# Mixer slices loaded channels-first from a second copy of the input, with the pooled product moved behind the fourth up tile

## Chip, cores and metric

The kernel runs on one core of a Trainium2 chip. The metric is the device time of one execution in microseconds (us), over several runs. The version before the change takes 1790.71 us (median of 3 runs, 1789.93 to 1791.59).

## What is computed

One layer (DEPTH is 1) of an encoder on two sequences of 2048 and 512 tokens, 1024 channels, in float32, with the same weights:

```
h = rms_norm(x, g_mix)
y = pool_mixer(h, pool_w, pool_scale)
x = x + y
x = x + relu(rms_norm(x, g_mlp) @ w_up)**2 @ w_down      # 1024 -> 4096 -> 1024
out = rms_norm(x, g_fin)

def pool_mixer(h, w, scale):          # four groups of 256 channels, windows 2, 4, 8, 16 tokens
    mean = (sum of h over the window centred on t) / (tokens in the window)
    d = mean - h                      # per channel group
    return einsum('bsgc,gce->bsge', d, w) * scale
```

## The kernel before

**Groups and steps.** The 2560 tokens are handled in five groups of 512 (`GT`). The hidden layer of a group is walked in eight steps (`PAIRS`) of 512 of its 4096 columns, so there are 40 steps. TensorE (PE) does in step n four *up tiles* 4n to 4n+3 (24 matmuls of 512 columns each: every f32 product is made of three, hi*hi, lo*hi and hi*lo, from operands split into a rounded high part and a rest) and, for the step before, the seven *products* of a Strassen scheme with w_down, in the order P1, P5, P6, P3, P4, P7, P2 (12 matmuls each, `product`, L1188 to L1190). ScalarE (ACT) takes the relu and the square of an up tile (L533, L535) and writes the high parts; VectorE (DVE) writes the low parts (L756, L765, L773), forms the Strassen sums (L785 to L817), and adds every finished product to its sum in SBUF (`evict`, L832). In the first group the split of w_down is made by DVE and ACT too (`split_w`, `sum_w`) and stored to DRAM; later groups load it back.

**The ring.** Products leave PE through a ring of two pairs of PSUM banks (`ring_pair`). `ring_turns` gives each product its turn; turns alternate between the pairs. A matmul group with turn r waits until turn r-2 has been read (`ring_read`), which only DVE does, in its own order.

**The mixer of the next group** is made during the steps of the present one. At step 2 of a group (`STATS_STEP`) SP loads the next group's rows `xr` and halo rows `xh`, ACT takes their mean squares (`row_stats`) and GpSimd (POOL) the factors `rs_x`. In steps 3 to 6 (`WINDOW_STEP` + w, w = 0 to 3) one channel group of 256 each is mixed:

- ACT multiplies the slice by the row factors into `xw` (`norm_rows`, L553, one step ahead), PE transposes it to channels by tokens with eight transposes ahead of the step's first up tile and two for the halo ahead of the second (`turn_window` L1198, `turn_halos` L1205), ACT copies the result from PSUM to `ht` (L562, L569);
- POOL adds shifted copies, w+1 adds of about 128x1024 for window w and a small multiplication at the sequence ends (`window_sums`, L347, L354);
- DVE subtracts the slice itself (`subtract_own`, L887), ACT writes the high part `dt_hi` (L573), DVE the low part `dt_lo` (L892);
- PE multiplies by the mixer weights: 24 matmuls of 256 columns into two turns of the ring, two halves of 256 tokens each (`pool_out`, L1213 to L1215);
- DVE adds both halves to `xr` (`add_pooled`, L875).

In step 7 the mixed rows are normalised, and at the boundary PE transposes them for the next group's up tiles. The first group has a path of its own, which the change leaves alone; so four groups by four windows, 16 *window steps*, are concerned.

**What sets the order.** The instructions of every engine are written out by hand in the `step` functions, one per engine, and each engine runs its own in that order. In a window step PE's `step` is

```
turn_window; up_tile(4n); P1; P5; turn_halos; up_tile(4n+1); P6; P3; up_tile(4n+2); P4; P7
pool_out
up_tile(4n+3); P2
```

Of PE's turns, the two halves of the pooled product lie between P7 and P2: P7's pair is the one of the second half, and P2 goes to the pair of the first half. SP issues the loads of rows, weights and mixer weights (`pw_slot`), ACT those of w_up (`load_wu`, behind each `split_wu`).

## Time and profile before

| | |
|---|---|
| median of 3 runs | 1790.71 us |
| profiled execution | 1790.22 us |
| its span in the trace | 1788.4 us |
| PE busy | 1756.3 us, 98% of the span |
| DVE busy | 1122.7 us, 63% |
| ACT busy | 761.4 us, 43% |
| POOL busy | 158.7 us, 9% |
| mean granted TensorE clock | 0.996 |
| DMA | 432.67 MB, mean 242 GB/s |

The busy times are those of one execution. Each engine's time is the union of its instructions, so 98% of PE says that hardly a moment passes without a matmul in flight; it does not say where an added wait would sit. The 1.8 us between the span and the time of that execution lie around the traced span. Consecutive matmuls overlap: a row's duration is longer than the distance to the next start, and it is the distance that costs time. The same holds for DVE and ACT, where the next start comes some 0.08 us ahead of an end.

### The profile page before, as it was taken

The page shows a single profiled execution, that of the slowest core. Times are in us where ns is not written, and L with a number is a line of the kernel's source. Part 1 is how long each engine was busy: PE and PEld are TensorE (multiplying, and loading weights), DVE is VectorE, ACT ScalarE, POOL GpSimd, SP SyncE. Part 2 cuts the span into 40 slices and gives each one's busy share as a digit, 9 for nine tenths or more (in the row PEclk, how much of TensorE's full clock was granted, in tenths as well). Part 3 has the DMA queues.
Part 4 walks back from the last instruction along what each step waited for, and adds up shares of the span by engine and source line. Part 5 has one row for each costly group of instructions (what it writes and reads, how often), then busy time and mean ns, then how long its engine had stood idle before and what let it go on. Part 6 is the DMA issues. An engine that isn't in the chain of part 4 may idle for free.

```text
span 1788.4 us, 20968 instructions
## 1 busy us (share of the span) xinstructions
PE 1756.3 (98%) x8156; PEld 1461.8 (82%) x8156; DVE 1122.7 (63%) x1178; ACT 761.4 (43%) x1186; POOL 158.7 (9%) x139
## 2 busy tenths in 40 slices
PE   8999999999999999999999999999999999999996
PEld 8888887778888888888888888888888888888885
DVE  6678888786555564765555647645556575445447
ACT  6556554554343335344333344343333543233232
POOL 4000112001001120010011200000112010000001
PEclk9999999999999999999999999999999999999998
DMA  7597766668856665668666555776665657666654
GB/s 266 218 348 281 265 252 242 245 263 326 307 212 224 223 224 212 247 242 295 243 223 223 213 212 204 280 295 223 224 224 212 235 205 273 240 223 239 233 202 163
DMA packets 80902, 432.67 MB, mean 242 GB/s; under 512 B 8860, under 2 KB 10780, under 8 KB 42916
## 3 DMA queue, kind: packets, MB, share of 16 engines
q1 hardware_dynamic: 57764, 347.44, 52.6%
q10 hardware_dynamic: 23040, 83.90, 13.8%
q8 instruction: 65, 1.06, 0.2%
q14 instruction: 33, 0.27, 0.0%
HBM read 360.00 MB, written 71.30 MB: 241 GB/s over the span
## 4 chain that ended last, share of the span: by engine, by line
PE 89%; DVE 6%; ACT 1%; DMA 1%; issue 1%; POOL 1%; ACTq 0%; SPq 0%; POOLq 0%; DVEq 0%
PE up_ps L1169 16%; PE up_ps L1171 16%; PE up_ps L1170 16%; PE ring_ps L1188 13%; PE ring_ps L1190 13%; PE ring_ps L1189 13%; DVE m_acc L832 1%; PE ring_ps L1213 1%; DVE w_slot L765 1%; PE ring_ps L1215 1%; PE ring_ps L1214 1%; DVE a_slot L773 1%; PE mix_ps L1198 1%; DVE wu_lo L756 1%; DMA wd_raw<-w_down 1%
## 5 line engine op out<-in xcount | busy, mean ns | idle before, releaser
L756 DVE TENSOR_TENSOR wu_lo<-wu_raw,wu_hi 128x1024 fp32r<-128x1024 f32 x158 | 195.8, 1239 | 579.7 <-ACT wu_hi L496 579.7
L1169 PE MATMUL up_ps<-h_hi,wu_hi 128*128 128x512 f32 x1280 | 501.4, 392 | 0.6 <-DVE h_lo L897 0.6
L1171 PE MATMUL up_ps<-h_hi,wu_lo 128*128 128x512 f32 x1280 | 498.5, 389 | 0.0
L1170 PE MATMUL up_ps<-h_lo,wu_hi 128*128 128x512 f32 x1280 | 498.5, 389 | 0.0
L533 ACT ACTIVATE a_raw<-up_ps 128x512 f32<-128x512 f32 x160 | 95.3, 596 | 509.0 <-PE up_ps L1171 509.0
L832 DVE TENSOR_TENSOR m_acc<-ring_ps,m_acc 128x1024 f32<-128x1024 f32 x245 | 298.6, 1219 | 18.8 <-PE ring_ps L1190 18.4
L1188 PE MATMUL ring_ps<-w_slot,a_slot 128*128 128x512 f32 x760 | 296.8, 391 | 1.1 <-DVE m_acc L832 1.1
L1190 PE MATMUL ring_ps<-w_slot,a_slot 128*128 128x512 f32 x760 | 295.9, 389 | 0.0
L1189 PE MATMUL ring_ps<-w_slot,a_slot 128*128 128x512 f32 x760 | 295.7, 389 | 0.0
L1171 PEld LDWEIGHTS up_ps<-h_hi,wu_lo 128*128 128x128 f32 x1280 | 240.2, 188 | 50.5
L1169 PEld LDWEIGHTS up_ps<-h_hi,wu_hi 128*128 128x128 f32 x1280 | 240.3, 188 | 49.4 <-DVE h_lo L897 1.2
L1170 PEld LDWEIGHTS up_ps<-h_lo,wu_hi 128*128 128x128 f32 x1280 | 240.4, 188 | 48.3
L525 ACT CAST a_slot<-s_sum 128x512 fp32r<-128x512 f32 x160 | 99.4, 621 | 278.4 <-PE ring_ps L1190 98.5
L1188 PEld LDWEIGHTS ring_ps<-w_slot,a_slot 128*128 128x128 f32 x760 | 142.6, 188 | 31.1 <-issue 1.5
L1190 PEld LDWEIGHTS ring_ps<-w_slot,a_slot 128*128 128x128 f32 x760 | 142.6, 188 | 29.9
L1189 PEld LDWEIGHTS ring_ps<-w_slot,a_slot 128*128 128x128 f32 x760 | 142.7, 188 | 29.2
L496 ACT CAST wu_hi<-wu_raw 128x1024 fp32r<-128x1024 f32 x160 | 165.4, 1034 | 0.0
L1188 PE MATMUL ring_ps<-w_more,a_slot 128*128 128x512 f32 x360 | 140.6, 391 | 0.1
L1190 PE MATMUL ring_ps<-w_more,a_slot 128*128 128x512 f32 x360 | 140.2, 389 | 0.0
L1189 PE MATMUL ring_ps<-w_more,a_slot 128*128 128x512 f32 x360 | 140.1, 389 | 0.0
L773 DVE TENSOR_TENSOR a_slot<-s_sum,a_slot 128x512 fp32r<-128x512 f32 x160 | 134.1, 838 | 3.4 <-ACT a_slot L525 3.4
L525 ACT CAST a_slot<-a_raw 128x512 fp32r<-128x512 f32 x120 | 74.5, 621 | 104.6 <-PE ring_ps L1190 104.5
(136 smaller groups left out, 1642.2 us busy)
## 6 DMA issues: line engine op xcount, KB each, us to landing
w_slot<-w_cache SPq DMA_DIRECT2D x134, 1024.0 KB, 5.1
w_more<-w_cache SPq DMA_DIRECT2D x90, 1024.0 KB, 5.1
wu_raw<-w_up ACTq DMA_DIRECT2D x160, 512.0 KB, 3.2
w_cache<-w_slot SPq DMA_DIRECT2D x56, 1024.0 KB, 4.9
wd_raw<-w_down SPq DMA_DIRECT2D x16, 1024.0 KB, 8.7
xr<-x SPq DMA_DIRECT2D x20, 512.0 KB, 7.6
out<-m_acc SPq DMA_DIRECT2D x20, 512.0 KB, 5.6
pw_slot<-pw_cache SPq DMA_DIRECT2D x16, 512.0 KB, 4.3
```

The source lines that it names most:

```text
L496: nc.scalar.copy(wu_hi[:, u % FT, :, :], wu_raw[:, u % FT, :, :]).then_inc(wu_hi_done, 1)
L525: nc.scalar.copy(a_slot[:, q % A_SLOTS, 0, :, :], a_source(q)).then_inc(a_hi_done, 1)
L533: nc.scalar.activation(a, up_ps[:, u % FT, :], ACT.Relu).then_inc(relu_done, 1)
L756: nc.vector.tensor_tensor(wu_lo[:, u % FT, :, :], wu_raw[:, u % FT, :, :], wu_hi[:, u % FT, :, :].bitcast(f32), ALU.subtract).then_inc(wu_ ...
L773: nc.vector.tensor_tensor(a_slot[:, i, 1, :, :], a_source(q), a_slot[:, i, 0, :, :].bitcast(f32), ALU.subtract).then_inc(a_lo_done, 1)
L832: nc.vector.tensor_tensor(dst, src, dst, ALU.add).then_inc(ring_read, 1)
L1169: nc.tensor.matmul(o, hi, h2_hi[:, d, :], start=(d == 0), stop=False)
L1170: nc.tensor.matmul(o, hi, h2_lo[:, d, :], start=False, stop=False)
L1171: last = nc.tensor.matmul(o, lo, h2_hi[:, d, :], start=False, stop=(d == DT - 1))
L1188: nc.tensor.matmul(dst, a_hi, hi, start=(k == 0), stop=False)
L1189: nc.tensor.matmul(dst, a_hi, lo, start=False, stop=False)
L1190: last = nc.tensor.matmul(dst, a_lo, hi, start=False, stop=(k == 1))
```

## The change

A second copy of the input, `x_turned`, is laid out on the host as channels by tokens, halo included (four groups, four windows, 128 x 2 x 528 values each). SP loads a window's slice straight into `xt`, which has two slots; `xw` and `ht` are gone, and with them `norm_rows`, `turn_window`, `keep_turned`, `turn_halos` and `keep_turned_halos`.

The slice arrives without its row factors. ACT now stores `rs_x` to a DRAM row in three pieces (`store_rs`, step 2), reads that row back one step later, broadcast to 128 partitions (`load_rs`, step 3), and POOL multiplies each slice by it, two instructions of 128x528 a window, in front of its adds (`next_sums`).

Two orders change as well. On PE `pool_out` now stands behind `up_tile(4n+3)`, straight ahead of P2. On DVE `subtract_own` and `split_pooled` stand behind the eviction of P7, and `add_pooled` behind `split_wu(4n+5)` and `sum_a(n, P5)`. On ACT `split_pooled` stands ahead of the last `split_w` and of `activate(4n+3)`. `ring_turns` is as before. POOL's `window_sums` of a window waits for the `dt_lo` of the window before, as the sums share two buffers.

```diff
+            def load_turned(m, w):
+                v = WINDOWS * (m - 1) + w
+                if v >= 2:
+                    sp.wait_ge(diff_done, v - 1)
+                sp.dma_start(xt[:, w % 2, :, :], x_turned[m - 1, w]).then_inc(xt_in[w % 2], 16)
...
                     load_ends(g + 1)
+                    load_turned(g + 1, 0)
+                    load_turned(g + 1, 1)
                     load_pool_w(g + 1, 0)
...
+                if mixes and WINDOW_STEP <= s < WINDOW_STEP + WINDOWS - 2:
+                    load_turned(g + 1, s - WINDOW_STEP + 2)
...
+            def store_rs(m):
+                act.wait_ge(rs_x_done, m)
+                row = rs_rows[m - 1]
+                act.dma_start(row[HALO:HALO + GT].rearrange("(j p) -> p j", p=P), rs_x[:, 0:TT],
+                              allow_slow_non_contiguous=True).then_inc(rs_stored, 16)
...
+            def load_rs(m):
+                act.wait_ge(rs_stored, 16 * ROW_PARTS * m)
+                if m > 1:
+                    act.wait_ge(xt_scaled, CT * WINDOWS * (m - 1))
+                act.dma_start(rs_b[:, :], rs_rows[m - 1].partition_broadcast(P)).then_inc(rs_b_in, 16)
...
-                if windows:
-                    keep_turned(g + 1, w)
                 activate(4 * n)
                 split_wu(4 * n + 2)
+                if mixes and s == WINDOW_STEP:
+                    load_rs(g + 1)
...
-                if windows:
-                    split_pooled(g + 1, w)
...
                 activate(4 * n + 2)
...
                 split_a(q0 + 7)
+                if windows:
+                    split_pooled(g + 1, w)
                 split_w(q0 + 8)
-                if mixes and 0 <= s - STATS_STEP < WINDOWS:
-                    norm_rows(g + 1, s - STATS_STEP)
+                if mixes and s == STATS_STEP:
+                    store_rs(g + 1)
                 activate(4 * n + 3)
...
@@ vector, step @@
-                if windows:
-                    subtract_own(g + 1, w)
-                    split_pooled(g + 1, w)
                 split_wu(4 * n + 4)
                 if n > 0:
                     evict(q0 + P4)
                     split_a(q0 + P2)
                     evict(q0 + P7)
+                if windows:
+                    subtract_own(g + 1, w)
+                    split_pooled(g + 1, w)
                 sum_w(n, P5)
                 split_w(q0 + NP + P1)
                 split_a(q0 + NP + P1)
-                if windows:
-                    add_pooled(g + 1, w)
                 split_w(q0 + NP + P5)
                 sum_w(n, P7)
                 sum_w(n, P6)
                 split_wu(4 * n + 5)
                 sum_a(n, P5)
+                if windows:
+                    add_pooled(g + 1, w)
...
@@ gpsimd @@
             def next_sums(m, w):
+                v = WINDOWS * (m - 1) + w
+                slot = xt[:, w % 2, :, :]
+                pool.wait_ge(xt_in[w % 2], 16 * (v // 2 + 1))
+                pool.wait_ge(rs_b_in, 16 * m)
+                for c in range(CT):
+                    nc.gpsimd.tensor_tensor(slot[:, c, :], slot[:, c, :], rs_b[:, :], ALU.mult).then_inc(xt_scaled, 1)
                 pool.wait_ge(ends_in, 16 * m)
-                pool.wait_ge(ht_done, TURNS * (WINDOWS * (m - 1) + w + 1))
-                window_sums(nc.gpsimd, pool, w, ht, sums, summed,
+                if v > 0:
+                    pool.wait_ge(dt_lo_done, v)
+                pool.wait_ge(xt_scaled, CT * (v + 1))
+                window_sums(nc.gpsimd, pool, w, slot, sums, summed,
                             SUM_STEPS[WINDOWS] * (m - 1) + SUM_STEPS[w])
...
@@ tensor, step @@
-                if windows:
-                    turn_window(g + 1, w)
                 up_tile(4 * n)
                 product(q0 + 0)
                 product(q0 + 1)
-                if windows:
-                    turn_halos(g + 1, w)
...
                 product(q0 + 5)
+                up_tile(4 * n + 3)
                 if windows:
                     pool_out(g + 1, w)
-                up_tile(4 * n + 3)
                 product(q0 + 6)
```

The order on DVE in a window step of a later group, from the split of up weights 4n+4 (`wu_lo`) over the evictions of P4 and P7 (`m_acc`) to that of P2, before:

```order
400 L756 TENSOR_TENSOR wu_lo<-wu_raw,wu_hi 128x1024
401 L832 TENSOR_TENSOR m_acc<-ring_ps,m_acc 128x1024
402 L773 TENSOR_TENSOR a_slot<-a_raw,a_slot 128x512
403 L832 TENSOR_TENSOR m_acc<-ring_ps,m_acc 128x1024
404 L773 TENSOR_TENSOR a_slot<-a_raw,a_slot 128x512
405 L875 TENSOR_TENSOR xr<-ring_ps,xr 128x2x256 x2
406 L756 TENSOR_TENSOR wu_lo<-wu_raw,wu_hi 128x1024
407 L809 TENSOR_TENSOR s_sum<-a_raw 128x512
408 L832 TENSOR_TENSOR m_acc<-ring_ps,m_acc 128x1024
```

and in the changed kernel:

```order
397 L761 TENSOR_TENSOR wu_lo<-wu_raw,wu_hi 128x1024
398 L837 TENSOR_TENSOR m_acc<-ring_ps,m_acc 128x1024
399 L778 TENSOR_TENSOR a_slot<-a_raw,a_slot 128x512
400 L837 TENSOR_TENSOR m_acc<-ring_ps,m_acc 128x1024
401 L892 SCALAR_TENSOR_TENSOR sums<-sums,xt 128x2x512
402 L897 TENSOR_TENSOR dt_lo<-sums,dt_hi 128x1024
403 L778 TENSOR_TENSOR a_slot<-a_raw,a_slot 128x512
404 L761 TENSOR_TENSOR wu_lo<-wu_raw,wu_hi 128x1024
405 L814 TENSOR_TENSOR s_sum<-a_raw 128x512
406 L880 TENSOR_TENSOR xr<-ring_ps,xr 128x2x256 x2
407 L837 TENSOR_TENSOR m_acc<-ring_ps,m_acc 128x1024
```

The difference and its low part came in behind P7's eviction, and the two additions of the pooled halves to `xr` now stand behind the split of up weights 4n+5 and one activation sum.

In a window step of the first group, which also splits w_down, the changed DVE order from P7's eviction on, with what each instruction waits for:

```order
129 L837 TENSOR_TENSOR m_acc<-ring_ps,m_acc 128x1024 [waits ring_full]
130 L892 SCALAR_TENSOR_TENSOR sums<-sums,xt 128x2x512 [waits summed]
131 L897 TENSOR_TENSOR dt_lo<-sums,dt_hi 128x1024 [waits dt_hi_done]
132 L790 TENSOR_TENSOR t_sum<-wd_raw 128x1024 [waits w_lo_done,raw_in0]
133 L770 TENSOR_TENSOR w_slot<-wd_raw,w_slot 128x1024 [waits w_hi_done]
134 L778 TENSOR_TENSOR a_slot<-a_raw,a_slot 128x512 [waits a_hi_done]
135 L770 TENSOR_TENSOR w_slot<-t_sum,w_slot 128x1024 [waits w_hi_done]
136 L794 TENSOR_TENSOR wd_raw<-wd_raw 128x2x512 [waits t_done,raw_in1]
137 L798 TENSOR_TENSOR t_sum<-wd_raw,t_sum 128x1024 [waits t_done,w_lo_done]
138 L761 TENSOR_TENSOR wu_lo<-wu_raw,wu_hi 128x1024 [waits wu_hi_done]
139 L814 TENSOR_TENSOR s_sum<-a_raw 128x512 [waits sq_done,a_lo_done]
140 L880 TENSOR_TENSOR xr<-ring_ps,xr 128x2x256 [waits ring_full] x2
```

Eight instructions stand between the low part of the difference and the additions; before, three of them did, and the low part itself came ahead of the evictions of P4 and P7.

On PE, the end of the pooled product in the changed kernel, and the first matmuls of P2 behind it:

```order
784 L1211 MATMUL ring_ps<-pw_slot,dt_hi 128x256
785 L1212 MATMUL ring_ps<-pw_slot,dt_hi 128x256
786 L1213 MATMUL ring_ps<-pw_slot,dt_lo 128x256
787 L1202 MATMUL ring_ps<-w_slot,a_slot 128x512 [waits ring_read,w_lo_done,a_lo_done]
788 L1203 MATMUL ring_ps<-w_slot,a_slot 128x512
```

Before, `up_tile(4n+3)` stood between the two.

## Rows read from the trace of the kernel before

**Rows 1.** The page, part 1: engine, busy us (share of the span), instructions

```profile
PE 1756.3 (98%) x8156; PEld 1461.8 (82%) x8156; DVE 1122.7 (63%) x1178; ACT 761.4 (43%) x1186; POOL 158.7 (9%) x139
```

**Rows 2.** Waits of PE, longest first: total us, times, longest us

```profile
PE ring_ps L1213 <- DVE m_acc L832: 5.7, 2, 4.0
```

**Rows 3.** Timeline of PE at a window step's transposes: start us, us, engine, line

```profile
144.88 0.39 PE L1190 MATMUL ring_ps<-w_slot,a_slot 128*128 128x512 f32 x1
145.11 1.03 PE L1198 MATMUL mix_ps<-ident,xw 128*128 128x128 f32 x8
...
146.22 0.40 PE L1170 MATMUL up_ps<-h_lo,wu_hi 128*128 128x512 f32 x1
...
156.65 0.39 PE L1190 MATMUL ring_ps<-w_slot,a_slot 128*128 128x512 f32 x1
...
157.34 0.39 PE L1170 MATMUL up_ps<-h_lo,wu_hi 128*128 128x512 f32 x1
```

**Rows 4.** Timeline of PE, third group: what follows an up tile; the pooled product

```profile
961.47 0.39 PE L1188 MATMUL ring_ps<-w_more,a_slot 128*128 128x512 f32 x1
...
977.79 0.28 PE L1213 MATMUL ring_ps<-pw_slot,dt_hi 128*128 128x256 f32 x1
...
980.80 0.40 PE L1169 MATMUL up_ps<-h_hi,wu_hi 128*128 128x512 f32 x1
```

**Rows 5.** Timeline of ACT in the same step

```profile
962.83 1.04 ACT L496 CAST wu_hi<-wu_raw 128x1024 fp32r<-128x1024 f32 x1
...
970.10 1.05 ACT L573 CAST dt_hi<-sums 128x1024 fp32r<-128x1024 f32 x1 [2.30 <-DVE sums L887]
```

**Rows 6.** Timeline of DVE in the same step

```profile
963.90 1.22 DVE L756 TENSOR_TENSOR wu_lo<-wu_raw,wu_hi 128x1024 fp32r<-128x1024 f32 x1 [1.80 <-ACT wu_hi L496]
...
968.85 1.22 DVE L887 SCALAR_TENSOR_TENSOR sums<-sums,ht 128x1024 f32<-128x1024 f32 x1
971.18 1.23 DVE L892 TENSOR_TENSOR dt_lo<-sums,dt_hi 128x1024 fp32r<-128x1024 f32 x1 [1.11 <-ACT dt_hi L573]
...
977.99 1.22 DVE L832 TENSOR_TENSOR m_acc<-ring_ps,m_acc 128x1024 f32<-128x1024 f32 x1 [0.25 <-PE ring_ps L1190]
979.13 0.68 DVE L773 TENSOR_TENSOR a_slot<-a_raw,a_slot 128x512 fp32r<-128x512 f32 x1
979.73 0.68 DVE L875 TENSOR_TENSOR xr<-ring_ps,xr 128x512 f32<-128x512 f32 x1
```

**Rows 7.** Timeline of DVE in a window step of the first group

```profile
184.40 1.22 DVE L765 TENSOR_TENSOR w_slot<-t_sum,w_slot 128x1024 fp32r<-128x1024 f32 x1
185.53 1.22 DVE L789 TENSOR_TENSOR wd_raw<-wd_raw 128x1024 f32<-128x1024 f32 x1
186.86 1.23 DVE L793 TENSOR_TENSOR t_sum<-wd_raw,t_sum 128x1024 f32<-128x1024 f32 x1
```

**Rows 8.** Groups of POOL's instructions: count, busy us, mean ns of one

```profile
L347 POOL TENSOR_TENSOR sums<-sums 128x1024 f32<-128x1024 f32 (+3 forms) x24 | 58.2, 2423 | 1.9
```

**Rows 9.** Timeline of POOL while DVE is busy, first group

```profile
298.88 7.94 POOL L347 TENSOR_TENSOR sums<-sums 128x1048 f32<-128x1048 f32 x3
```

**Rows 10.** Timeline of DVE in the same stretch

```profile
301.62 2.94 DVE L765 TENSOR_TENSOR w_slot<-t_sum,w_slot 128x1024 fp32r<-128x1024 f32 x1
304.48 3.42 DVE L756 TENSOR_TENSOR wu_lo<-wu_raw,wu_hi 128x1024 fp32r<-128x1024 f32 x1
```

**Rows 11.** Table by stretch of 4 us: busy of PE, PEld, DVE, ACT, POOL, then PEclk

```profile
270.00:274.00 4.00, 2.79 (x21) 2.64 (x22) 4.00 (x5) 1.60 (x3) 0.00 (x0) 1.00 1.01 423
...
316.00:320.00 4.00, 0.54 (x3) 0.11 (x1) 3.13 (x3) 2.98 (x5) 0.00 (x0) 1.00 0.99 336
320.00:324.00 4.00, 3.51 (x17) 3.54 (x18) 4.00 (x5) 1.79 (x3) 0.00 (x0) 0.57 1.02 426
```

**Rows 12.** The page, part 6: DMA issues with KB each, us to landing

```profile
xh<-halos SPq DMA_DIRECT2D x4, 64.0 KB, 8.8
```

More of the change, by code:

```diff
@@ L546, in row_stats @@
                     mean_square(src, ms_x[0:rows, j:j + 1], rows).then_inc(ms_x_done, 1)
-            def norm_rows(m, w):
+            def store_rs(m):
                 act.wait_ge(rs_x_done, m)
-                c = slice(w * WC, (w + 1) * WC)
-                for j in range(NORMS):
-                    rows, src = (P, xr[:, j, c]) if j < TT else (2 * HALO, xh[:, c])
-                    nc.scalar.activation(xw[0:rows, j, :], src, ACT.Copy,
-                                         scale=rs_x[0:rows, j:j + 1]).then_inc(xw_done, 1)
@@ L1408 @@
     pw_cache = nc.dram_tensor("pw_cache", (WINDOWS, P, 2, CT * WC), mybir.dt.float32, kind="Internal").ap()
-    build(nc, *args, w_cache, pw_cache, out)
+    rs_rows = nc.dram_tensor("rs_rows", (GROUPS - 1, HT), mybir.dt.float32, kind="Internal").ap()
+    build(nc, *args, w_cache, pw_cache, rs_rows, out)
     r = run_bass_kernel_spmd(nc, [arrays], core_ids=[0])
```

67 lines of the change are left out of this document (22 added, 45 removed).

## Prediction

> **What bounds the kernel.** I read the busy shares first: TensorE (PE) works 98% of the span [rows 1], so a matmul taken away is time won, and a gap put between matmuls is time lost. Then PE's waits: in the steady part it waits for DVE just twice in front of the pooled product, 5.7 us together, the longer 4.0 us [rows 2]. So the four other engines are hidden now, and the question is whether they still are when the orders change. For that I read, step by step, the timelines of PE, ACT and DVE in one window step of a later group [rows 4 to 6], of DVE in the first group, where it also splits w_down [rows 7], and of POOL and DVE together [rows 9, 10].
>
> **Part 1: transposes out of PE.** The eight transposes stand between starts at 145.11 and 146.22; a lone matmul needs 0.23, so they cost 0.88. The two halo transposes make 0.69 out of two distances of 0.23: 0.23 us [rows 3]. 16 window steps x 1.11 = **17.8 us off**. All of it is on PE, nothing covers it.
>
> **Part 2: waits that go.** The two waits ahead of the pooled product were for the evictions of P4 and P7, which stood behind the difference on DVE. DVE now evicts both first, and the pooled product comes an up tile later: **5.7 us off**. After the 4.0 us wait the granted clock is 0.57 over four microseconds, between the levels 2.4 and 1.2 GHz, while around the shorter wait it stays 1.00 [rows 11]; (1 - 0.57) x 4 = **1.7 us off**. The second half's bank was also free a moment late: 24 matmuls of 256 columns take 3.01 us [rows 4] where I count 2.86 without that hitch: 16 x 0.15 = **2.4 us off**. Gains together: 27.6 us.
>
> **Part 3: the wait that comes.** P2 uses the pair of banks of the pooled product's first half, and may start only when DVE has added that half to `xr`. Before, a whole up tile lay between the two on PE. Now P2 follows at once, while `add_pooled` on DVE has moved behind `split_wu(4n+5)`. That split needs the high part that ACT writes when up tile 4n+3 is complete, and behind it `sum_a` needs that tile's square. So nothing of the chain can begin before the pooled product does.
>
> *A later group, POOL quiet (window 3).* Count from the start of what follows an up tile, 961.47 [rows 4]. The high part starts at 962.83 [rows 5], the low part at 963.90 [rows 6]: 2.43. It holds DVE 1.13 (a distance in [rows 7]), `sum_a` 0.60 (a 512-column operation, 979.13 to 979.73, [rows 6]), the half's addition 0.68, 0.07 until PE sees it (estimated; ACT's end at 963.87 to DVE's start at 963.90 is 0.03, [rows 5, 6]): P2 could start at 4.91. PE is free at 2.86. **Wait 2.05 us.**
>
> *First group, POOL quiet.* Zero is now the start of up tile 4n+3. P7's eviction starts at 0.20 and the next instruction 1.14 later [rows 6]: the difference at 1.34. The low part starts 2.33 after it (968.85, 970.10 on ACT, 971.18) [rows 5, 6]: 3.67, complete at 4.90, ahead of PE's need at 24 x 0.23 = 5.5. Then DVE has eight instructions: w sum 4.81, split 5.95, a split 7.09, split 7.69, w sum 8.83, w sum 10.16 (1.33 behind, [rows 7]), `split_wu` 11.30, `sum_a` 12.43, addition 13.03 to 13.71, P2 at 13.8. PE is free at 5.5 + 2.86 = 8.4. **Wait 5.4 us.** ACT is earlier than DVE throughout: its `dt_hi` is over at 3.7, and its delayed split, activation and high part end by 9.3.
>
> *POOL in the chain.* POOL now waits for `dt_lo` of one window, complete at 4.9, to begin the sums of the next. In windows 0, 1 and 2 that puts 2, 3 and 4 big additions right beside the chain. What this does [rows 9, 10]: while three such additions run, a DVE subtraction of two SBUF operands takes 2.94 or 3.42 instead of 1.22 us, so 1.7 to 2.2 more; the two engines take turns. I take 2.0 for each addition. First group: 9 additions (2+3+4) x 2.0 = 18 us, all in front of some DVE instruction of the eight, on top of 4 x 5.4 = 21.6: **39.6 us**. Later groups: only `split_wu` and `sum_a` can be held. POOL's second addition spans about 7.5 to 9.7, `split_wu` is ready at 7.9 and goes 1.7 late; in windows 1 and 2 the third addition slips in ahead of `sum_a`, 2.2 more. Waits 3.75, 5.95, 5.95 and 2.05, 17.7 a group, three groups: **53.1 us**. Window 3 is undisturbed, since no sums follow it.
>
> The Trainium skill, page "SBUF — State Buffer", section "SBUF: two separate sides", calls the port pair of DVE and GpSimd an exclusive lock, which whoever comes first holds for its whole instruction. The rows agree in kind. Read strictly, each hold would be a whole POOL addition, 2.42 us in the mean [rows 8]; the 9 first-group holds would then add 9 x 0.42 = 3.8 us and those of a later group 2.6 (3 x 0.72 on `split_wu`, 2 x 0.22 on `sum_a`), 7.8 in three, and the sum would be 1884 instead of 1872.
>
> *Clock.* A wait of 4.0 us was followed by a loss of 1.7 us, one of 1.7 us by none [rows 2, 11]. Ten of the new waits are longer than 4.0 (four in the first group, six later): 10 x 1.7 = **17 us**. The three of 3.75 I count at nothing, with 5 us as their upper bound.
>
> **Part 4: what costs nothing.** ACT, at 43% [rows 1], loses work and gets three stores and a load a group; nothing on it is near PE's need except what is timed above. POOL gets 32 multiplications of 528 columns, about half an addition or 1.2 us each, 38 us on an engine at 9%; those for windows 0 and 1 run in step 3 ahead of the difference, and those for 2 and 3 wait for a load issued only when the first-group chain is nearly over. If one falls into it, it is 1 to 2 us more, in the upper bound. SP: the mixer weights' load waits for the pooled product's second half, now an up tile later, but the load behind it waits for P2 anyway; 16 slices of 540 KB add 2% to the traffic. The pooled product's own weights were loaded a step ahead.
>
> **Sum.** Against the profiled execution of 1790.2 us (0.5 under the median): 1790.2 - 27.6 + 39.6 + 53.1 + 17 = **1872 us**, slower by 82 us or 4.6%.
>
> **Rivals.**
>
> *A: the wait comes, POOL does not get into it.* If POOL's additions are over, or yield, before DVE's chain needs the port, waits are 4 x 5.4 and 12 x 2.05 = 46.2, and only the first group's four cost clock, 6.8: 1790.2 - 27.6 + 53.0 = 1816. For it: in the first group the overlap [rows 9, 10] lay at another place of the step. Against: POOL's start is tied to `dt_lo`, the same instruction behind which the chain begins. Between A and the forecast lie cases where only some additions hold. 0.13 in all.
>
> *B: P2 is not held.* Then only the gains stay: 1790.2 - 27.6 = 1763, faster. It decides at one point: the first half must be added within 2.86 us of the pooled product's start, and the shortest chain is 4.9 us [rows 4 to 6]. It could be so if DVE reached the addition ahead of `split_wu`, against the written order. 0.03.
>
> *C: the row factors come late.* Stored and read back through DRAM, they let POOL start the first window of each group only when they are there. The load is issued after the first activation of step 3, about 8 us into it; the difference is due some 34 us in, and multiplications and sums take about 8. That leaves 18 us for a transfer; a small load takes 8.8 us to land [rows 12]. Were it 10 us over, four windows would pay 10 each, 1912 us. The skill's "DMA: Bandwidth & Descriptors", section "Specifications", wants 512 bytes a piece for full rate, and this store is made of 4-byte pieces; no row here shows such a store. 0.03.
>
> *D: no net change,* if the chain were so short that waits just eat the 27.6 us, 1790. It would take waits of 1.7 us a window without clock loss, less than the shortest I find. 0.01.
>
> **How the numbers follow.** The forecast has 0.80. Its own spread: a hold of 1.7 or 2.42 instead of 2.0 (-7 to +10), clock losses for 7 or 13 waits or up to twice as long (-5 to +20), first-group chain partly hidden (-20): 1838 to 1905. To leave out no more than 2 in 10 I stretch the low end towards A, to 1825. A measurement of this kernel can tell 0.2%, 3.6 us, from no change. Faster by more: B, 0.03. Within: 0.01. Slower by more: 0.96.
>
> **What would show it.** On PE, L1198 and L1205 gone, and in the waits a new one, P2's first matmul (L1202) for DVE's addition to `xr` (L880), 16 times, 90 us in all, 2 us in window 3 of later groups, 9 us and over in the first. DVE's `split_wu` and `sum_a` behind the difference at 2 to 3.4 us instead of 1.2 and 0.7 in windows 0 to 2. PEclk below 1.00 after the long waits. A sum of L1202's waits near 46 us says A, none says B; POOL idle for long on `rs_b`, with DVE's L892 waiting on POOL, says C.

## The result, and the profile after

The changed kernel takes **1884.84 us** in the median of 6 runs (1883.66 to 1887.03); the kernel before, in 6 runs, 1790.91 (1789.73 to 1791.69). The ratio is 1.0526, 95% interval 1.0513 to 1.0540: slower by 5.3%. The forecast was 1872 us, range 1825 to 1905. The changed kernel's trace is of the execution of 1883.66 us.

The head of the page of the changed kernel, with its chain by engine:

```profile
span 1881.9 us, 20602 instructions
PE 1768.1 (94%) x7996; PEld 1467.0 (78%) x7996; DVE 1115.7 (59%) x1177; ACT 712.6 (38%) x1058; POOL 210.8 (11%) x171
PEclk9999888999999999999999999999999999999998
...
PE 82%; DVE 8%; issue 3%; ACT 3%; DMA 3%; ACTq 0%; POOL 0%; POOLq 0%; SPq 0%; DVEq 0%
```

PE has lost four points of its share [rows 1], and its busy time holds matmuls at the lower clock too. What it waits for, in the view of waits (us in total, times, longest):

```profile
PE ring_ps L1202 <- DVE xr L880: 84.0, 16, 12.8
PE mix_ps L1235 <- DVE h_lo L902: 4.2, 5, 2.4
...
PE ring_ps L1211 <- DVE dt_lo L897: 2.3, 1, 2.3
PE ring_ps L1202 <- DVE a_slot L778: 2.1, 3, 1.2
```

The first line is P2's wait for the pooled product's first half to be added, once in each of 16 window steps. The waits for evictions ahead of the pooled product [rows 2] are gone. The second line is the group boundary's, and stands outside the window steps. The timeline of PE, at that wait in windows 0 and 2 of the first group and in windows 1 and 3 of the next (wait in brackets):

```profile
200.66 0.76 PE L1202 MATMUL ring_ps<-w_slot,a_slot 128*128 128x512 f32 x1 [9.27 <-DVE xr L880]
...
316.56 0.77 PE L1202 MATMUL ring_ps<-w_slot,a_slot 128*128 128x512 f32 x1 [12.77 <-DVE xr L880]
...
641.21 0.77 PE L1202 MATMUL ring_ps<-w_slot,a_slot 128*128 128x512 f32 x1 [4.96 <-DVE xr L880]
...
740.02 0.47 PE L1202 MATMUL ring_ps<-w_more,a_slot 128*128 128x512 f32 x1 [2.01 <-DVE xr L880]
```

All four windows of the first group: 9.27, 10.61, 12.77 and 5.42 us; of the next: 3.29, 4.96, 5.04 and 2.01. Window 3 is the shortest in both groups, as POOL has nothing to sum there. How POOL gets into the chain is read from DVE's timeline in windows 2 and 3 of that next group:

```profile
686.46 2.52 DVE L761 TENSOR_TENSOR wu_lo<-wu_raw,wu_hi 128x1024 fp32r<-128x1024 f32 x1 [2.37 <-ACT wu_hi L507]
688.90 2.40 DVE L814 TENSOR_TENSOR s_sum<-a_raw 128x512 f32<-128x512 f32 x1
691.23 1.27 DVE L880 TENSOR_TENSOR xr<-ring_ps,xr 128x512 f32<-128x512 f32 x2
...
737.45 1.23 DVE L761 TENSOR_TENSOR wu_lo<-wu_raw,wu_hi 128x1024 fp32r<-128x1024 f32 x1 [2.37 <-ACT wu_hi L507]
738.59 0.69 DVE L814 TENSOR_TENSOR s_sum<-a_raw 128x512 f32<-128x512 f32 x1
739.19 1.28 DVE L880 TENSOR_TENSOR xr<-ring_ps,xr 128x512 f32<-128x512 f32 x2
```

It is the same chain, high part, low part, `sum_a`, addition, in both. In window 2, `split_wu` takes 2.52 instead of 1.23 and `sum_a` 2.40 instead of 0.69, 3.0 us together, which is the difference of the two waits (5.04 and 2.01). POOL's timeline in window 2:

```profile
683.62 2.27 POOL L347 TENSOR_TENSOR sums<-xt 128x1052 f32<-128x1052 f32 x1 [39.52 <-DVE dt_lo L897]
685.97 7.57 POOL L347 TENSOR_TENSOR sums<-sums 128x1048 f32<-128x1048 f32 x3
```

Its additions lie across exactly those two DVE instructions, and each of these waits for one of them. The Trainium skill, page "SBUF — State Buffer", section "SBUF: two separate sides", calls the port that the two engines share an exclusive lock; the trace agrees in kind.

The clock. Windows of four microseconds behind the wait of 9.27 us and around that of 2.01 us; PEclk is the third number from the end (busy times of PE, PEld, DVE, ACT, POOL, then PEclk, DMA share, GB/s):

```profile
202.00:206.00 4.00, 4.00 (x13) 3.14 (x12) 0.34 (x1) 0.26 (x1) 2.32 (x2) 0.63 0.15 62
...
738.00:742.00 4.00, 1.99 (x7) 1.63 (x7) 2.47 (x4) 0.00 (x0) 0.00 (x0) 0.85 0.22 90
742.00:746.00 4.00, 4.00 (x14) 3.16 (x13) 1.36 (x2) 0.62 (x1) 0.00 (x0) 0.72 0.18 25
```

Behind the short wait too the clock falls to its lower level. Matmul by matmul, in PE's timeline behind the first wait (the matmul at 202.07 and the last of P2):

```profile
202.07 0.63 PE L1202 MATMUL ring_ps<-w_slot,a_slot 128*128 128x512 f32 x1
202.50 0.63 PE L1203 MATMUL ring_ps<-w_slot,a_slot 128*128 128x512 f32 x1
...
205.00 0.40 PE L1203 MATMUL ring_ps<-w_slot,a_slot 128*128 128x512 f32 x1
205.23 0.39 PE L1204 MATMUL ring_ps<-w_slot,a_slot 128*128 128x512 f32 x1
```

A distance of 0.43 us is the level of 1.2 GHz, 0.23 that of 2.4. For every wait I took the distances of the 30 matmuls behind it and added up what each has over 0.227: first group 2.08, 2.84, 2.19, 2.10; second 1.58, 2.01, 2.17, 1.74; third 1.50, 1.95, 2.09, 1.72; fourth 1.48, 1.94, 2.13, 1.73. All 16 waits cost clock, **31.2 us** together. This sum is called the clock loss of a wait from here on.

With it the account, from span to span: 1788.4 - 27.6 (transposes, old waits, their clock, bank) + 84.0 + 31.2 + 2.3 + 2.1 (the two small new waits) = 1880.4, against 1881.9. The rest stands at the first group boundary: behind PE's wait of 2.41 us there (419.77) the granted clock is 0.57 over four microseconds, which costs 1.7 us, and behind the same wait of the kernel before, 1.94 us, it stays at 1.00. The 27.6 is the prediction's own figure; how far it holds is said below.

### The profile page after: what moved, and what is told of

Read it like the earlier page. It is cut to its first block, busy times and chain, and to the rows that moved or that the text cites. A ratio compares the mean times of both kernels' runs of the same rounds, so it can differ in the third digit from the quotient of the medians.

```text
span 1881.9 us, 20602 instructions
## 1 busy us (share of the span) xinstructions
PE 1768.1 (94%) x7996; PEld 1467.0 (78%) x7996; DVE 1115.7 (59%) x1177; ACT 712.6 (38%) x1058; POOL 210.8 (11%) x171
## 4 chain that ended last, share of the span: by engine, by line
PE 82%; DVE 8%; issue 3%; ACT 3%; DMA 3%; ACTq 0%; POOL 0%; POOLq 0%; SPq 0%; DVEq 0%
PE up_ps L1183 14%; PE up_ps L1185 14%; PE up_ps L1184 14%; PE ring_ps L1202 13%; PE ring_ps L1203 12%; PE ring_ps L1204 12%; DVE w_slot L770 1%; DVE s_sum L814 1%; DVE m_acc L837 1%; DMA wd_raw<-w_down 1%; ACT wu_hi L507 1%; DVE a_slot L778 1%; DMA w_cache<-w_slot 1%; DMA wu_raw<-w_up 1%; DVE wu_lo L761 1%
## 5 line engine op out<-in xcount | busy, mean ns | idle before, releaser
L761 DVE TENSOR_TENSOR wu_lo<-wu_raw,wu_hi 128x1024 fp32r<-128x1024 f32 x158 | 205.8, 1302 | 611.8 <-ACT wu_hi L507 611.8
L1202 PE MATMUL ring_ps<-w_slot,a_slot 128*128 128x512 f32 x760 | 308.1, 405 | 68.6 <-DVE xr L880 65.3
L1203 PE MATMUL ring_ps<-w_slot,a_slot 128*128 128x512 f32 x760 | 304.0, 400 | 0.0
L1204 PE MATMUL ring_ps<-w_slot,a_slot 128*128 128x512 f32 x760 | 303.5, 399 | 0.0
L1202 PEld LDWEIGHTS ring_ps<-w_slot,a_slot 128*128 128x128 f32 x760 | 148.1, 195 | 103.5 <-issue 68.8
L1204 PEld LDWEIGHTS ring_ps<-w_slot,a_slot 128*128 128x128 f32 x760 | 147.6, 194 | 32.0
L1203 PEld LDWEIGHTS ring_ps<-w_slot,a_slot 128*128 128x128 f32 x760 | 148.4, 195 | 30.4
L1202 PE MATMUL ring_ps<-w_more,a_slot 128*128 128x512 f32 x360 | 145.0, 403 | 18.8 <-DVE xr L880 18.7
L1203 PE MATMUL ring_ps<-w_more,a_slot 128*128 128x512 f32 x360 | 143.2, 398 | 0.0
L1204 PE MATMUL ring_ps<-w_more,a_slot 128*128 128x512 f32 x360 | 143.0, 397 | 0.0
L778 DVE TENSOR_TENSOR a_slot<-s_sum,a_slot 128x512 fp32r<-128x512 f32 x160 | 110.5, 690 | 3.4 <-ACT a_slot L536 3.4
```

The costliest lines, as they stand in the source:

```text
L761: nc.vector.tensor_tensor(wu_lo[:, u % FT, :, :], wu_raw[:, u % FT, :, :], wu_hi[:, u % FT, :, :].bitcast(f32), ALU.subtract).then_inc(wu_ ...
L778: nc.vector.tensor_tensor(a_slot[:, i, 1, :, :], a_source(q), a_slot[:, i, 0, :, :].bitcast(f32), ALU.subtract).then_inc(a_lo_done, 1)
L1202: nc.tensor.matmul(dst, a_hi, hi, start=(k == 0), stop=False)
L1203: nc.tensor.matmul(dst, a_hi, lo, start=False, stop=False)
L1204: last = nc.tensor.matmul(dst, a_lo, hi, start=False, stop=(k == 1))
```

## Experiments

The main theory: the time goes to P2's wait for `add_pooled`, which stands too late on DVE and is made longer by POOL's additions; and to the half clock behind it. Rivals: that POOL, not the place, makes the wait; that the lower clock comes from something other than the wait; that the new data path (slices by DMA, POOL's multiplications, the stored factors) costs time of its own. Single runs are one execution with a profile; "the kernel before" was run beside each, and its median stayed within 1790 to 1792.

### The addition early again

```diff
                 split_a(q0 + NP + P1)
+                if windows:
+                    add_pooled(g + 1, w)
                 split_w(q0 + NP + P5)
...
                 sum_a(n, P5)
-                if windows:
-                    add_pooled(g + 1, w)
```

> The changed kernel with one edit: on DVE the addition of the pooled halves goes back to its old place, behind the low part of P1's activations and ahead of the split of P5's weights; PE's order stays changed. Theory (the place of the addition makes the wait): in later groups DVE then reaches the addition at 5.5 us after up tile 4n+3 begins and waits there for the product; the first half is added by about 7.7, P2 is due at 8.4, so PE's wait for it is 0 in all 12 later windows and in window 3 of the first group, and 3 to 5 us in windows 0 to 2 of the first group, where two of POOL's additions still come in ahead of it. Sum 10 to 14 us of waits instead of 84, and clock loss for three waits instead of 16: 1774 to 1786 us, faster than the kernel before. Rival (DVE and POOL together have too much to do in these steps, wherever the addition stands): DVE's work is the same, so the waits move to other instructions and the time stays above 1850 us.

Measured: 1785.96 us (8 runs), ratio to the kernel before 0.9973 (0.9962 to 0.9984), at the upper end of what was expected. PE's wait for the addition:

```profile
PE ring_ps L1202 <- DVE xr L880: 9.4, 3, 3.6
```

Moving one call takes 99 us off the changed kernel and makes a small gain of it. The wait is left in windows 0 to 2 of the first group alone (2.35, 3.52 and 3.57), where the additions of POOL still stand beside three DVE instructions ahead of the call. So the place of the call is the cause, and in the later groups POOL alone does not make the wait.

### POOL's sums held back, the addition late

```diff
                 pool.wait_ge(ends_in, 16 * m)
+                if w > 0:
+                    pool.wait_ge(ring_read, TURN[(m, w - 1, 1)] + 1)
```

> The changed kernel with one wait added on POOL: the sums of the next window begin only when DVE has added both pooled halves of this one, so no large POOL addition lies beside DVE's chain; orders as in the change. Theory (POOL's additions lengthen the chain by taking turns with DVE): waits of P2 become 5.4 us in each of the four first-group windows and 2.0 us in each of the twelve later ones, 46 us instead of 84, DVE's split of up weights in the chain back to 1.2 us; with half clock behind each wait as now (about 1.7 us) the time is 1845 to 1850 us. Rival (POOL is beside the point, DVE is late in windows 0 to 2 for its own work): the waits stay at 84 us and the time within 2 us of 1885.

Measured: 1843.01 us (one run), 2 us under what was expected. PE's first wait:

```profile
PE ring_ps L1204 <- DVE xr L880: 44.8, 16, 5.4
```

With POOL out of the chain (the sums begin only when the pooled product's second half has been read) the waits are 4.38 and three of 5.42 in the first group, and 2.01 or 2.02 twelve times: the two quiet values of the prediction, 5.4 and 2.05, summing to 44.8 where it had 46.2. DVE's timeline in window 2 of the first group shows both engines apart:

```profile
299.77 1.22 DVE L761 TENSOR_TENSOR wu_lo<-wu_raw,wu_hi 128x1024 fp32r<-128x1024 f32 x1
300.90 0.68 DVE L814 TENSOR_TENSOR s_sum<-a_raw 128x512 f32<-128x512 f32 x1
```

POOL's share of the wait is therefore 84.0 - 44.8 = 39.2 us. The clock loss is 9.7 us for the four long waits; of the twelve short ones ten lose 1.68 to 1.74 and two lose 0.1, as a P2 without a fall of the clock does too. This is the pair in PE's timeline, the ninth to eleventh matmul behind a wait of 2.02 us, first one that lost, then one that did not:

```profile
625.80 0.63 PE L1204 MATMUL ring_ps<-w_slot,a_slot 128*128 128x512 f32 x1
626.23 0.63 PE L1205 MATMUL ring_ps<-w_slot,a_slot 128*128 128x512 f32 x1
...
672.42 0.40 PE L1206 MATMUL ring_ps<-w_slot,a_slot 128*128 128x512 f32 x1
672.66 0.39 PE L1204 MATMUL ring_ps<-w_slot,a_slot 128*128 128x512 f32 x1
```

### The wait filled with transposes

PE gets so many transposes of `ident` into the free `mix_ps` that they cover most of the wait; nothing reads them. The wait's length should stay, the clock should not fall.

```diff
+FILL = ((80, 92, 112, 48), (28, 44, 44, 16))
...
                     pool_out(g + 1, w)
+                    for i in range(FILL[min(g, 1)][w]):
+                        nc.tensor.transpose(mix_ps[:, i % 2, 0:P], ident[:, :], ident[:, :])
                 product(q0 + 6)
```

> The changed kernel with dummy work: ahead of P2 in each window step PE makes 16 to 112 transposes of the identity into a PSUM bank that nobody reads in these steps, about as long as the wait was (0.11 us each). Theory (31 us of the change's cost is the granted clock, which falls in the wait and stays at half for the first of P2's matmuls): the chain on DVE is as long as before, but PEclk stays at 1.00 and P2's twelve matmuls take 2.7 us instead of 4.2 to 5.3; time 1853 to 1858 us, 27 to 31 below the changed kernel. Rival (the first matmuls after a wait are slow for another reason, as operands fetched late, and the clock follows the wait only): P2 stays at 4.2 us and over, and the time does not fall.

Measured: 1855.61 us (one run). What is left of the wait, in the view of waits:

```profile
PE ring_ps L1203 <- DVE xr L881: 4.0, 15, 0.6
```

The first fill in PE's timeline:

```profile
194.33 8.89 PE L1306 MATMUL mix_ps<-ident 128*128 128x128 f32 x80
```

And the windows view of the stretch that had a clock of 0.63 in the changed kernel:

```profile
202.00:206.00 4.00, 4.00 (x25) 3.50 (x23) 0.69 (x3) 0.00 (x0) 0.03 (x1) 1.00 0.60 237
```

From the last matmul of the pooled product to the first of P2 it is as long as in the changed kernel, to 0.05 us, in 15 of the 16 windows; in the first it is 0.8 us shorter, 8.77 instead of 9.55. P2's twelve matmuls, which took 4.2 to 5.3 us in the changed kernel, take 2.8 in all 16, 29 us less in sum. The kernel is 29 us faster: this is the clock, measured apart from the wait. No clock loss behind a filled wait is over 0.2 us.

### The new data path alone

PE, ACT and DVE get the order of the kernel before (`pool_out` ahead of `up_tile(4n+3)`, the difference ahead of `split_wu(4n+4)`, the addition behind `split_a` of P1'); slices, factors and POOL stay as changed. Shown are the new places only; the same calls go out at the places that they have in the changed kernel, and ACT's `split_pooled` goes back ahead of `activate(4n+2)`.

```diff
                 if windows:
+                    subtract_own(g + 1, w)
+                    split_pooled(g + 1, w)
                 split_wu(4 * n + 4)
...
                 split_a(q0 + NP + P1)
+                if windows:
+                    add_pooled(g + 1, w)
...
                 if windows:
                     pool_out(g + 1, w)
+                up_tile(4 * n + 3)
                 product(q0 + 6)
```

> The new data path alone: slices loaded channels-first, row factors through DRAM, POOL's multiplications, no transposes; but PE's, DVE's and ACT's orders as in the kernel before. Theory (the whole loss comes from the orders, and the transposes were worth 17.8 us): 1773 us, up to 1785 if POOL's sums, which now begin right behind the low part of the last window's difference, delay the evictions of P4 and P7 in the first group. Rival (the data path costs too, by POOL's 46 us of multiplications beside DVE or by the loads): over 1791 us.

Measured: 1795.88 us (7 runs), ratio 1.0028 (1.0017 to 1.0039). Slower than the theory's range; the expectation's rival, over 1791, held. The view of waits, then a later group's window 1 on POOL and on DVE:

```profile
PE ring_ps L1211 <- DVE m_acc L837: 22.1, 22, 5.8
```

```profile
582.40 1.92 POOL L347 TENSOR_TENSOR sums<-xt 128x1036 f32<-128x1036 f32 x1 [26.49 <-DVE dt_lo L897]
584.40 4.75 POOL L347 TENSOR_TENSOR sums<-sums 128x1032 f32<-128x1032 f32 x2
...
584.65 2.74 DVE L761 TENSOR_TENSOR wu_lo<-wu_raw,wu_hi 128x1024 fp32r<-128x1024 f32 x1 [2.38 <-ACT wu_hi L507]
```

The sums used to wait for the turned slice; now the slice is early, so they begin at once behind `dt_lo`. There they hold `split_wu(4n+4)`, and the evictions of P4 and P7 behind it come late, 22 times. The transposes' gain is spent again by an engine that has become faster to start.

### Both causes out, in the new order and in the old

The first kernel holds POOL's multiplications and sums back as above and has the addition early; the second has the same hold and the old orders.

```diff
                 slot = xt[:, w % 2, :, :]
+                if w > 0:
+                    pool.wait_ge(ring_read, TURN[(m, w - 1, 1)] + 1)
                 pool.wait_ge(xt_in[w % 2], 16 * (v // 2 + 1))
```

> The additions of the pooled halves at their old place on DVE, as in e1_add_early, and POOL's multiplications and sums of windows 1 to 3 only after DVE has added the pooled halves of the window before. Theory (the last 9.4 us of waits of e1_add_early are POOL's turns with DVE in the first group): P2's waits for the addition fall to 0, with the 6.6 us of half clock behind them; the 2.4 us for the first window's low part and the 3 us in step 3 stay or shrink: 1786 - 16 = 1770 us, 1767 to 1773, over 1% faster than the kernel before. Rival (these waits are DVE's own work in the first group, which also splits w_down): no more than 3 us are won, 1783 us or over.

Measured: 1780.82 us (5 runs), ratio 0.9941 (0.9929 to 0.9953), 11 us above the middle of what was expected. The waits for the addition are gone, but another has come in the view of waits:

```profile
PE ring_ps L1204 <- DVE a_slot L778: 9.6, 5, 2.8
```

Three of the five stand in the first group's windows, 2.42, 2.69 and 2.77 us. POOL now takes turns with the DVE instructions behind the addition (in the first window four of them take 2.2 to 2.9 us each, beside POOL's multiplications and sums from 193.35 on), and these prepare P1' and P5'. The hold moved POOL from one late chain to the next.

> The orders of the kernel before with the new data path, as in e6_old_orders, and POOL held back as in e7_early_and_late. Theory (the 22 us of waits of e6_old_orders come from POOL's sums, which begin right behind the low part and hold up the evictions of P4 and P7): those waits go, but for the 2 us that the kernel before had of itself, and the time is the old one less the transposes, 1773 us (1770 to 1777). Then the new places of the pooled product and of the difference are needed only because of where POOL works. Rival (the old orders cannot feed the pooled product once slices come by DMA): time stays at 1790 to 1796.

Measured: 1776.81 us (4 runs), ratio 0.9917 (0.9902 to 0.9932), as expected. PE's waits in the steady part are 2.1 us once for `a_slot`, and:

```profile
PE ring_ps L1213 <- DVE m_acc L837: 5.3, 2, 3.7
```

Against the kernel before that is 14.5 us off: the data path pays, with none of the order changes. And the same data path and hold with PE's and ACT's new orders, and on DVE the late difference with the early addition (1780.82), is 4 us behind it; the two sets of runs do not overlap, the intervals of the two ratios do a little.

### The transposes put back

The first of those two kernels, with eight unread transposes ahead of `up_tile(4n)` and two ahead of `up_tile(4n+1)`, to price their removal by itself.

```diff
                 windows = g < LAST and 0 <= w < WINDOWS
+                for i in range(8 if windows else 0):
+                    nc.tensor.transpose(mix_ps[:, i % 2, 0:P], ident[:, :], ident[:, :])
                 up_tile(4 * n)
...
```

> e7_early_and_late with eight dummy transposes ahead of a window step's first up tile and two ahead of the second, into a bank that nobody reads there: PE's part of the removed work alone, 160 transposes. Theory: 16 x (0.88 + 0.23) = 17.8 us over e7_early_and_late. Rival (in the old kernel part of their time was cover for other engines, so that removing them gained less): 12 us or less.

Measured: 1793.87 us (10 runs), so they cost 13.05 us, between the 17.8 of the theory and the 12 of the rival. PE's view of waits says where part of the difference is:

```profile
PE ring_ps L1204 <- DVE a_slot L778: 6.5, 6, 1.9
```

9.6 have become 6.5: 3.1 us of the transposes stood where PE would have waited. The clock has the rest: in the steady part of the run without them the granted clock falls to 0.50 four times (at 188, 205, 301 and 386 us), in the run with them twice (252 and 386), each fall costing 1.6 to 1.7 us, 3.2 us together. With both, less some 1 us of small waits that grew, the transposes come to 18 us, as the theory had them. Why the clock fell less often is not shown.

### The pooled product back, the difference late

The early addition, and `pool_out` ahead of `up_tile(4n+3)` again.

```diff
-                up_tile(4 * n + 3)
                 if windows:
                     pool_out(g + 1, w)
+                up_tile(4 * n + 3)
```

> e1_add_early with the pooled product back ahead of up tile 4n+3 on PE, everything else as there. The low part of the difference is complete 4.9 us after P7's matmuls, so PE waits that long at the pooled product in all 16 window steps, in the first group up to 7: 75 to 90 us of waits for the low part, and none for the addition, as an up tile lies between. With 1.7 us of half clock behind each wait: 1783 + 78 + 27 - 12 = 1876 us. A rival that puts the change's loss down to the pooled product's new place expects less than 1786.

Measured: 1887.84 us (one run), 12 us over the expectation.

```profile
PE ring_ps L1211 <- DVE dt_lo L897: 79.6, 16, 7.9
```

7.9 us in the first window and 4.8 in each of the 15 others, 4.9 forecast. The pooled product's place and the difference's place belong together: with the difference behind the evictions, the up tile between has to cover its chain. What was missed is once more the clock: behind each of the 16 waits the matmuls' distances lose 2.3 to 2.6 us, 39 us in sum where 27 was expected. Its mean is 0.967, as in the changed kernel's 0.968.

### The stored row factors

In all of these kernels but the last one, where it is 7.9 us, one wait of 2 to 6 us is left in the first window or ahead of it. Part of it leads back to ACT's queue. In the changed kernel, ACT's timeline in the step before the windows:

```profile
143.91 0.39 ACTq L563 DMA_DIRECT2D rs_rows<-rs_x  x1
...
146.13 0.37 ACTq L499 DMA_DIRECT2D wu_raw<-w_up  x1
...
158.32 1.05 ACT L507 CAST wu_hi<-wu_raw 128x1024 fp32r<-128x1024 f32 x1 [4.62 <-DMA wu_raw<-w_up]
```

and in the windows view, while the store is being worked on:

```profile
148.00:152.00 4.00, 4.00 (x19) 3.33 (x18) 4.00 (x4) 1.02 (x2) 0.00 (x0) 1.00 0.60 25
152.00:156.00 4.00, 4.00 (x18) 3.10 (x17) 3.74 (x5) 1.67 (x3) 0.00 (x0) 1.00 0.81 290
```

The store writes 512 factors of 4 bytes. At a busy share of 0.60 the DMA engines moved 25 GB/s, and the w_up slice issued behind it on the same queue landed 12.2 us later, where the median of the 160 is 3.6. The Trainium skill, page "DMA: Bandwidth & Descriptors", section "Specifications", gives 512 bytes as the least transfer for full rate; the 25 GB/s of this store agree in kind. Three kernels test it, all from the second of the pair above (1776.81 us; its slice lands after at most 13.0 us).

*The store twice,* the second copy to a row that nothing reads:

```diff
-                act.dma_start(row[HALO:HALO + GT].rearrange("(j p) -> p j", p=P), rs_x[:, 0:TT],
+                for copy in (row, rs_rows[GROUPS - 1 + m - 1]):
+                    act.dma_start(copy[HALO:HALO + GT].rearrange("(j p) -> p j", p=P), rs_x[:, 0:TT],
...
```

> e8_old_orders_late with the large of the three row-factor stores made twice, the second into a row that nobody reads. Theory (the 4-byte store is the cost): the up weights' load behind it lands some 8 us later still, about 20 us after issue in the first group; with 2 us of wait at PE now and a slack of a few us in the later groups, PE waits 8 to 10 us more in the first group and 2 to 6 in each later one, with half clock behind: 1790 to 1805 us. Rival (no cost of the store): 1777 us.

Measured: 1795.31 us (6 runs), ratio 1.0026 (1.0014 to 1.0038), 18.5 us more. The slice lands after up to 19.7 us, 6.7 later, and:

```profile
167.63 1.04 ACT L507 CAST wu_hi<-wu_raw 128x1024 fp32r<-128x1024 f32 x1 [12.73 <-DMA wu_raw<-w_up]
```

So the store's time in the queue is what makes this load late, and one copy stood just at the edge of what the schedule hides.

*The store behind the slice's load:*

```diff
-                if mixes and s == STATS_STEP:
-                    store_rs(g + 1)
                 activate(4 * n + 3)
                 split_wu(4 * n + 5)
+                if mixes and s == STATS_STEP:
+                    store_rs(g + 1)
```

> e8_old_orders_late with the three stores of the row factors issued one place later on ACT, behind the activation and the load of up weights that follow, so that the next such load comes a whole up tile later and not at once. Theory (the store of 4-byte pieces keeps the DMA engines busy at 25 to 31 GB/s for some 8 us; the up weights' load issued 2 us behind it lands after 12 us instead of 3.6, and ACT, DVE and PE wait in turn in step 3 of the first group): the waits at 164 and 186 us of that run, 2.1 and up to 3.7 us with 1.7 us of half clock, go or halve: 1770 to 1774 us. Rival (these waits come from POOL's first multiplications beside DVE): no change, 1776 to 1778.

Measured: 1777.58 us (5 runs), ratio 0.9930 (0.9917 to 0.9942): no gain, a miss, and it lies where the expectation's rival had it. ACT now waits at another place, in `load_rs`, which stands ahead of its other work and needs the store complete; the wait is booked to the next instruction:

```profile
161.86 0.62 ACT L536 CAST a_slot<-s_sum 128x512 fp32r<-128x512 f32 x1 [4.73 <-DMA rs_rows<-rs_x]
```

*The store earlier,* behind `split_wu(4n+4)`, right after the factors exist:

```diff
                 split_wu(4 * n + 4)
+                if mixes and s == STATS_STEP:
+                    store_rs(g + 1)
                 split_a(q0 + 6)
...
                 split_w(q0 + 8)
-                if mixes and s == STATS_STEP:
-                    store_rs(g + 1)
                 activate(4 * n + 3)
```

> e8_old_orders_late with the stores of the row factors issued half an up tile's work earlier on ACT, behind the load of up weights 4n+5 and some 8 us ahead of the next such load, instead of 2 us ahead of it. Theory (e10_store_behind_load only moved the wait, from the up weights' load to the load of the factors, which must wait for the store itself): with 8 us behind it and 15 us until the factors are read back, neither waits; the up weights land in under 5 us, PE's 2.1 us at 164 us with 1.7 us of half clock go, and the 3.7 us at 186 shrink, since the first window's multiplications start 4 us earlier: 1770 to 1773 us. Rival (these waits are POOL's turns with DVE in step 3, not the store): 1776 to 1778 us.

Measured: **1773.90 us** (4 runs), ratio 0.9903 (0.9886 to 0.9919), the fastest of all, faster than the kernel before by 1.0%; it lies 0.9 us above the expected range and 2 us below the rival's. ACT's waits for a late slice are down to 3.6 us in two, PE's wait for `a_slot` to 1.1. The gain over the kernel without this edit is 2.9 us, and the intervals of the two ratios overlap: that this last edit helps is likely, not shown. One wait stays open:

```profile
PE ring_ps L1213 <- DVE m_acc L837: 5.8, 2, 4.2
```

4.2 of it are in the first window, whose evictions are late though the slice now comes nearly in time. The rival of this expectation and of the one before, POOL's first turns with DVE, has its part here. Ahead of that window POOL's first two multiplications and its first sum run beside DVE:

```profile
163.04 3.36 POOL L1126 TENSOR_TENSOR xt<-xt,rs_b 128x528 f32<-128x528 f32 x2 [24.98 <-DMA rs_b<-rs_rows]
...
163.49 1.72 DVE L822 TENSOR_TENSOR s_sum<-a_raw 128x512 f32<-128x512 f32 x1
...
167.40 2.91 DVE L761 TENSOR_TENSOR wu_lo<-wu_raw,wu_hi 128x1024 fp32r<-128x1024 f32 x1
```

With the instruction between them (2.35 instead of 1.22) three of DVE's take 3.8 us more than undisturbed, and from there to the evictions DVE is idle for 2.0 us only, around the difference. So in this window two causes add up, the late load and POOL's first turns, and taking the first away leaves the second. That was read from the trace and not tried by a run of its own.

## Why the prediction was right, and where its sum was off

The forecast case is what happened: slower, through P2's wait for the addition, with POOL in its chain. The median is 13 us above the forecast.

**Part 1, transposes, 17.8 us.** PE has 160 fewer of them; put back they cost 13.05 in a kernel that still waits a little. 3.1 us of the difference had cover there and 3.2 are lower clock that the other run had more of, so the price on PE is right; "nothing covers it" is not, in a kernel that waits.

**Part 2, the old waits, 9.8 us.** The two waits are gone [rows 2], with the lower clock behind the longer one. The bank's hitch can be read from the traces: from the first to the last start of the pooled product's 24 matmuls it was 2.89 us in 12 of the 16 windows and over that in the others, and is 2.71 in all but the first now, some 3 us in sum where 2.4 was taken.

**Part 3, the wait.** Its place and both quiet lengths were right: 5.4 and 2.05 us forecast, 5.4 and 2.0 measured with POOL held back. With POOL: first group 9.27, 10.61, 12.77 and 5.42, together 38.1 where 39.6 was taken; later groups 15.3 a group where 17.7 was taken, 45.9 in three against 53.1. So the holds were mis-sized: in the later groups 1.3 us on `split_wu` and 1.7 on `sum_a` (window 2, above), where I took 1.7 and 2.2 from the longest rows of before [rows 10]. In sum 84.0 instead of 92.7. The strict reading of the Trainium skill's lock rule gave 1884 as a total, near the median, but by larger holds, and the holds came out smaller than mine: that its total fits is chance.

**The clock, the term that failed.** I counted 1.7 us for each of ten waits over 4.0 us and nothing for the shorter, since the one wait of 1.7 us in the kernel before cost nothing [rows 2, 11]. Measured were 31.2 us instead of 17. Both halves of the step were short: the six waits of 2.0 to 3.3 us lost 1.48 to 1.74 each, 9.7 us together, and the ten long ones 2.1 on average. Two points, a wait that cost and one that didn't, had been made a threshold at the upper of them. The filled wait shows that it is the clock: 29 us with the wait's length as it was. That the forecast came within 13 us all the same is in part luck: the holds were taken 8.7 us too long, which hid as much of the clock's error.

**Part 4, costs at nothing.** POOL's multiplications measured 1.46 us in the mean instead of 1.2. Ahead of the first window they and the first sum lengthen three DVE instructions (1.70, 2.91 and 2.36 us, from 166.00 on) by 3.9 us; of PE's waits in the changed kernel at most 0.35 us follows from them directly. The factors (rival C) landed 6.5 us after their load in the median, and PE never waited for a window's sums. But a cost was missed there: the 4-byte store delays the next load on its queue. In the changed kernel that shows as waits of 2.1 us for `a_slot`. The 2.3 us for `dt_lo` have more behind them: ACT's `dt_hi` stands behind a split that waits 6.55 us for its slice of w_down, and SP issued that load only at 176, behind a store that waited for a split of DVE's; DVE was late by the w_up slice and by POOL's turns. No run separates the two there. In the fast variants the store's place decides between 1774 and 1777 us at most, and doubled it costs 18.5. "SP, ACT: nothing near PE's need" was true of ACT's instructions, not of its queue.

**The rivals.** A would have been 1816 with a wait of 46.2 us: the kernel with POOL held back has that wait (44.8) and takes 1843, so A's price was short by the same clock term, 26.9 us where it had 6.8. B needs the first half added within 2.86 us and D waits of 1.7; the shortest waits measured were 2.0. Rival C's 1912 did not come either: the factors were there.

The errors of the sum: holds -8.7, clock +14.2, small new waits +4.4. With them 1872.3 becomes 1882.2, and the profiled execution took 1883.7; 1.7 us of lower clock at the first group boundary, which the kernel before did not have, cover the rest. The range's own terms (-7, -5, -20 and +10, +20) give 1840 to 1902, and not 1838 to 1905, and the 1 to 2 us of Part 4 do not close both ends; nothing hangs on it.

## What to carry to other kernels

When a result is moved later on PE, look at who needs its buffer next and whether the instruction that frees it has moved by as much: here the matmuls were given an up tile more, and the addition that frees the bank was put behind a chain that starts only then. An engine that becomes ready earlier is no gain by itself: the sums that start earlier took DVE's turns at the worst place, so hold it to a place where nothing waits for DVE. And price a gap on PE by its length plus some 2 us of lower clock, also when the gap is only 2 us, though not every such gap pays it; work put in the gap, if only transposes, saves the second part.

## What the runs showed of the hardware

- **Gaps of 2.0 us are mostly followed by the lower clock.** In the changed kernel all three such waits for the addition, with POOL held back ten of twelve, were followed by matmuls at 0.43 us instead of 0.23, at a loss of 1.7 us; two of the same length and place lost nothing. The length alone does not decide: the changed kernel's wait of 2.3 us at 188.29 and one of 2.7 us with both causes out (254.28) lost nothing, and one of 1.8 us with the transposes put back (252.02) was followed by 1.7 us of loss. What tells them apart is open. Longer gaps cost little more: 1.9 to 2.9 us behind 5 to 13 us. Behind the long ones the lower level is there at once; behind the ten of 2.0 us that lost, with POOL held back, it was there at once four times and came after three to five matmul distances at the higher level in the other six (the one shown above is of these).
- **The two engines take turns, one instruction each.** DVE's subtraction takes 2.5 to 2.9 us and its 512-column sum 2.4, against 1.22 and 0.68, one POOL addition for each. Additions whose operand is in PSUM do not seem to be held (1.27 for two halves at 691.23, right behind two held ones; 1.28 undisturbed).
- **A store of 512 factors of 4 bytes holds up the loads on its queue.** In the first group the 512 KB load behind it lands after 12.2 or 13.0 us, where the median of all is 3.6 and no other of the changed kernel takes over 10.1; with the store made twice it takes 19.7, 6.7 more. With the store moved ahead (1773.90 us) the load issued just before it took 12.1.
